# A hybrid decoder layer: weight rooms at other addresses, convolution taps spread over two steps, four rooms for the first token tiles, dt later

## The reference

```python
u = rms_norm(x, norm_pre_w)                          # (2048, 1024)
proj = u @ w_in                                      # q k v g z x b c dt
q, k, v, g, z, xbc, dt = split(proj)                 # 4*1024, 1024, 1024+512, 16
attn = mixture_of_dilations(q * 64**-0.5, k, v) * silu(g)   # windows 128, 512, 2048; dilations 1, 4, 16
xbc = silu(causal_depthwise_conv(xbc, conv_w) + conv_b)     # 4 taps along the tokens
dt = softplus(dt + dt_bias)
y = ssd_chunked(xs, dt, -exp(a_log), b, c) + d_skip * xs    # state-space scan, chunks of 128
y = gated_group_rms_norm(y, z, ssm_norm_w)
out = x + rms_norm(concat(attn, y) @ w_out, norm_post_w)
```

## Time and profile before

| | before |
|---|---|
| median of 3 runs | 2313.26 us (2310.68 to 2316.27) |
| profiled execution: time, span | 2307.99 us, 2306.2 us |
| mean granted clock of TensorE | 0.977 |
| TensorE matmuls busy | 2177.1 us, 94% |
| VectorE busy | 1413.7 us, 61% |
| ScalarE busy | 997.9 us, 43% |
| GpSimd busy | 1443.9 us, 63% |
| HBM over the span | 120 GB/s |

### The profile page before, as it was taken

How to read it: one execution, slowest core, us unless ns; L and a number is a source line. 1 busy time by engine, 2 the same in 40 slices (tenths; PEclk the granted TensorE clock), 3 DMA queues, 4 the chain that set the end, 5 groups by cost and what they waited for, 6 DMA issues and landing times. The chain is left out here.

```text
span 2306.2 us, 34733 instructions
## 1 busy us (share of the span) xinstructions
PE 2177.1 (94%) x12061; PEld 1835.2 (80%) x12061; DVE 1413.7 (61%) x2605; ACT 997.9 (43%) x2341; POOL 1443.9 (63%) x877
## 2 busy tenths in 40 slices
PE   5999999989999999998989999999996699999998
PEld 3778877777888888877858999999996588888876
DVE  6462236995522223499657777777777866666661
ACT  5332343333422234333336777777774423323231
POOL 6577677888667767788815556556542455555552
PEclk8999999999999999999989999999998799999999
DMA  4463332333733233322455555565547343444431
GB/s 129 151 230 105 92 106 61 108 92 128 237 107 108 97 92 110 92 73 83 137 126 114 144 126 133 139 158 137 139 115 260 103 130 128 138 129 131 140 100 55
DMA packets 260220, 287.19 MB, mean 125 GB/s; under 512 B 78420, under 2 KB 228112, under 8 KB 251984
## 3 DMA queue, kind: packets, MB, share of 16 engines
q1 hardware_dynamic: 258944, 277.50, 41.2%
q0 software_dynamic: 1104, 7.47, 0.8%
HBM read 195.28 MB, written 81.00 MB: 120 GB/s over the span
## 5 line engine op out<-in xcount | busy, mean ns | idle before, releaser
L935 PE MATMUL mm<-b_hi,w_hi 128*128 128x512 f32 x1456 | 576.3, 396 | 7.0 <-DVE fm L757 4.9
L937 PE MATMUL mm<-b_hi,w_lo 128*128 128x512 f32 x1456 | 573.0, 394 | 0.0
L936 PE MATMUL mm<-b_lo,w_hi 128*128 128x512 f32 x1456 | 572.5, 393 | 0.0
L493 POOL TENSOR_TENSOR w_lo<-w_raw,w_hi 128x512 fp32r<-128x512 f32 x208 | 315.3, 1521 | 132.1 <-ACT w_hi L567 123.9
L935 PEld LDWEIGHTS mm<-b_hi,w_hi 128*128 128x128 f32 x1456 | 274.0, 188 | 70.2 <-issue 9.4
L937 PEld LDWEIGHTS mm<-b_hi,w_lo 128*128 128x128 f32 x1456 | 273.9, 188 | 62.8
L936 PEld LDWEIGHTS mm<-b_lo,w_hi 128*128 128x128 f32 x1456 | 274.1, 188 | 61.3
L1729 PE MATMUL ps_t<-ident_b,probs 128*128 128x128 f32 x1136 | 214.6, 279 | 13.9 <-ACT probs L1660 6.8
L567 ACT ACTIVATE w_hi<-w_raw 128x512 fp32r<-128x512 f32 x208 | 129.2, 627 | 214.0 <-PE mm L937 209.2
L2214 PE MATMUL ps_out<-wo_hi,mix_hi 128*128 128x512 f32 x512 | 208.7, 408 | 1.3 <-ACT mix_hi L2165 1.3
L757 DVE SCALAR_TENSOR_TENSOR fm<-mm,u 128x512 f32<-128x512 f32 x120 | 92.0, 769 | 184.8 <-PE mm L937 184.6
(11 more groups left out here) (236 smaller groups left out, 4443.4 us busy)
## 6 DMA issues: line engine op xcount, KB each, us to landing
w_raw<-in_w_in_dram SPq DMA_DIRECT2D x52, 1024.0 KB, 5.7
feat<-fm SPq DMA_DIRECT2D x56, 512.0 KB, 5.5
tok<-tok_tile SPq DMA_DIRECT2D x52, 512.0 KB, 4.1
raw_q<-feat SPq DMA_DIRECT2D x32, 512.0 KB, 6.3
raw_k<-feat SPq DMA_DIRECT2D x32, 512.0 KB, 6.5
cum_b<-cum_scratch SPq DMA_DIRECT2D x16, 1024.0 KB, 7.8
cls_nat<-cls_out SPq DMA_DIRECT2D x64, 132.0 KB, 2.7
tok_tile<-in_x_dram SPq DMA_DIRECT2D x16, 512.0 KB, 3.8
```

The source lines that it names most:

```text
L493: pool.tensor_tensor(wl[o][:, :, :], source(o, n), wh[o][:, :, :].bitcast(F32), ALU.subtract)\
L935: pe.matmul(bank, w_hi[:, k, :], bh[o][:, k, :], start=(opens and k == 0), stop=False)
L936: pe.matmul(bank, w_hi[:, k, :], bl[o][:, k, :], start=False, stop=False)
L937: last = pe.matmul(bank, w_lo[:, k, :], bh[o][:, k, :], start=False, stop=(closes and k == KH - 1))
```

## The change

- **Rooms.** `TANH_AT` loses its 32 bytes, and with it all that is placed above it. Rooms 4 and 5 move to `SLOT_AT`, 112 KB. `dt_late` moves into the second half of a token room (T3).
- **Orders.** New strings put a v, k or q step behind most convolved steps. The feature set of each step is written out in `SETS`.
- **Taps.** The step behind a convolved one runs the first tile's four taps, tanh and finish, the step after that the second tile's (`conv_behind`). Each tile is turned by itself: `turn_at` is (n + 2, 0) and (n + 3, 0) for convolved steps, (n + 1, 3) for both tiles of v and z. `free_fm`, `turned` and `tok_made` count by tile.
- **Token tiles.** `x_room` has four rooms, two of them in `raw[1]`. Tiles 0 to 3 are loaded at once, 4 to 7 behind the first normalisations, and the second weights only behind the last turned part. `PREP` starts at step 0.
- **Reload.** Places (25, 1), (25, 3), (25, 4), (25, 6) and (26, 0) to (26, 2); six rows are loaded at step 24, sixteen at 25, six at 26 (ten, sixteen and two before).
- **dt.** `take_size` and `take_one_plus` run at s = 1 and s = 5, `take_ratio` at 5, `take_softplus` at 10, `cumulate` at 13; on ScalarE `dt_exps` at p = 2 and `dt_log` at p = 7.

```diff
-TANH_AT = CONV_AT + 8 * KB + 32
+TANH_AT = CONV_AT + 8 * KB
...
-ORDERS = ("qqqqkkvvvvzzzzxxxxbcggggkk", "qqqqkkkkvvvvzzzzxxxxbcgggg")
+ORDERS = ("qqqqxvxkxvxkbvckvzzzzggggk", "qxqxqxqxkbkckkvvvvzzzzgggg")
+SETS = ("00000101010101011010101010", "01010101010100010101010101")
...
-        self.set = 0 if n < 6 else n % 2
+        self.set = int(SETS[half][n % len(SETS[0])])
+        self.turn_at = [(n + 2 + b, 0) for b in range(2)] if self.conv else [(n + 1, 3)] * 2
...
+        SLOT_AT = sb.at
+        sb.at += 8 * KB
...
-        for rooms, group in ((sb, (4, 5)), ...
+        for rooms, group in ((Rooms(nc, SLOT_AT, SLOT_AT + 8 * KB), (4, 5)), ...
...
-        dt_out = [fm1[1], place(nc, "dt_late", dt_late_at, [P, HALF])]
+        dt_out = [fm1[1], place(nc, "dt_late", T3 * 16 * KB + 8 * KB, [P, HALF])]
+        x_wide = raw[1][:, :, :].rearrange("p k f -> p (k f)")
+        x_rooms = [*x_tok, x_wide[:, 0:D_MODEL], x_wide[:, D_MODEL:2 * D_MODEL]]
...
-        RELOAD = {(TURN - 1, 1): 0, (TURN - 1, 2): 1, (TURN - 1, 3): 2, (TURN - 1, 5): 3, (TURN, 0): 4, (TURN, 1): 5,
+        RELOAD = {(TURN - 1, 1): 0, (TURN - 1, 3): 1, (TURN - 1, 4): 2, (TURN - 1, 6): 3, (TURN, 0): 4, (TURN, 1): 5,
                   (TURN, 2): 6}
-        PREP = {j + 1: j for j in range(LANES)}
+        PREP = {j: j for j in range(LANES)}
...
+        def conv_behind(n):
+            if n and steps[n - 1].conv:
+                return steps[n - 1], 0
+            if n > 1 and steps[n - 2].conv:
+                return steps[n - 2], 1
+            return None
...
-                for i in range(2, 6):
-                    sp.wait_ge(normed, i - 1)
+                for i in range(4, HT):
+                    sp.wait_ge(normed, i - 3)
                     load_x(i)
-                load_w(1)
...
+                sp.wait_ge(u_turned, START)
+                load_w(1)
...
                     if conv:
-                        bring(conv)
+                        if conv[1] == 0:
+                            bring(conv[0])
                         for j in range(CONV_K):
-                            tap_step(conv, 0, j)
+                            tap_step(*conv, j)
...
                     read(s, A12, put(s, 0, 0), c1[:, :])
-                    if conv:
-                        tap_step(conv, 1, 0)
-                        tap_step(conv, 1, 1)
...
                     if conv:
-                        finish(conv, 0)
-                        tap_step(conv, 1, 2)
-                        tap_step(conv, 1, 3)
+                        finish(*conv)
...
-                        if s == 4:
+                        if s == 1:
+                            take_size()
+                        if s == 5:
+                            take_one_plus()
                             take_ratio()
-                        if s == 8:
+                        if s == 10:
                             take_softplus()
-                        if s == 12:
+                        if s == 13:
                             cumulate()
...
+                    if is_first(pair) and p == 2:
+                        dt_exps()
+                    if is_first(pair) and p == 7:
+                        dt_log()
```

More of the change, by code:

```diff
@@ L159, in all_steps @@
             out.append(Step(len(out), half, kind, FIRST_PAIR[kind] + order[:i].count(kind), out[:]))
+    for s in out:
+        s.turn = [sum(t.turns and t.turn_at[b] < s.turn_at[b] for t in out) for b in range(2)]
     return out
@@ L243, in project @@
         prep_out = sem("prep_out")
-        stage_in = [sem(f"stage_in{i}") for i in range(len(stage))]
+        rows_in = [sem(f"rows_in{i}") for i in range(len(stage))]
+        X_LOADS = [6, 6, 2, 2]
         u_turned = sem("u_turned")
@@ L267, in project @@
         conv_done = sem("conv_done")
-        turned = sem("turned")
-        tok_made = sem("tok_made")
+        turned = [sem(f"turned{b}") for b in range(2)]
+        tok_made = [sem(f"tok_made{b}") for b in range(2)]
         tok_out = [sem(f"tok_out{b}") for b in range(2)]
@@ L313, in bank, with due, free_fm @@
             return mm[(PRODUCTS * s.n + o) % BANKS]
-        def free_fm(eng, s):
+        def due(n, o):
+            return [(s, b) for s in steps if s.turns for b in range(2) if s.turn_at[b] == (n, o)]
+        def conv_behind(n):
[4 more added lines that the diff above has]
+            return None
+        def free_fm(eng, s, b):
             m = s.before
@@ L320, in free_fm @@
             if m is not None and m.turns:
-                eng.wait_ge(turned, 4 * (m.turn + 1))
+                eng.wait_ge(turned[b], 2 * (m.turn[b] + 1))
             if s.n == first_one:
@@ L359, in store_fm, with store_tok @@
                     sp.dma_start(dst, src).then_inc(fm_out[s.set], 16)
[L361 to L365, removed]
+                def store_tok(s, b):
+                    sp.wait_ge(tok_made[b], 2 * s.turn[b] + 2)
+                    sp.dma_start(tok_view[:, s.half * HT:(s.half + 1) * HT, (s.pair * 2 + b) * P:(s.pair * 2 + b + 1) * P],
+                                 tok[b][:, :, :]).then_inc(tok_out[b], 16)
                 def store_rows(j):
@@ L422, in _ @@
                             store_fm(last, b)
[L423 to L426, removed]
+                    for part in due(n, 0):
+                        store_tok(*part)
                     if n in PREP:
@@ L653, in _ @@
                     square(i + 2)
[L654 to L657, removed]
+                    high(i, 0)
+                square(6)
+                square(7)
+                high(4, 0)
                 for j in range(LANES):
@@ L675, in _ @@
                             square(HT + 2 * PREP[n] + half)
+                    conv = conv_behind(n)
                     if n:
                         read_first(s)
[L678 to L682, removed]
+                    high(0, n + 1)
+                    for part in due(n, 0):
+                        collect(*part)
                     reload(n, 0)
                     high(1, n + 1)
[L685 to L688, removed]
                     reload(n, 1)
@@ L697, in _ @@
                     high(4, n + 1)
-                    if last is not None and last.conv:
-                        conv_tanhs(last, 1)
+                    reload(n, 4)
                     high(5, n + 1)
-                    reload(n, 5)
                     high(6, n + 1)
+                    reload(n, 6)
                     if s.gz:
@@ L859, in _ @@
                     last = steps[n - 1] if n else None
-                    conv = last if last is not None and last.conv else None
+                    conv = conv_behind(n)
                     if n in PREP:
@@ L1053, in _ @@
                             multiply(s, o)
-                        if o == 0 and last2 is not None and last2.conv and last2.turns:
-                            turn_tiles(last2)
-                        if o == 0 and last is not None and last.kind == "v":
-                            turn_tiles(last)
-                        if o == 1 and last is not None and last.kind == "z":
-                            turn_tiles(last)
+                        for part in due(n, o):
+                            turn_tile(*part)
                         reload(n, o)
```

170 lines of the change are left out of this document (90 added, 80 removed).

## The result

The changed kernel takes 2249.88 us (median of 4 runs, 2247.75 to 2251.10) against 2314.56 for the kernel before in the same runs; the ratio is 0.9722, with a 95% interval of 0.9705 to 0.9739. In a second comparison it was 2250.65 against 2310.79, 0.9739 (0.9726 to 0.9753). So it is 60 to 65 us faster; the prediction was 2255.7, a gain of 57.6.

The account below looks back on a forecast made before the run. TensorE was taken as full outside the convolved stretches and VectorE as the bound of the steps behind convolved ones; the terms sum to -57.6 from the 2313.26 median, giving 2255.7 us, range 2243 to 2268 (8 in 10: 2241 to 2280).

Parts of the forecast that it names:

- Rooms, -16: Weight rooms moved to whole KB: 208 of 364 products 0.07 to 0.08 us faster, 13 to 17 us over 52 steps.
- rival 1: Address plays no part; products are slow by their place in the step: gain 38.1 us, time 2275, chance 0.09.
- Output projection, -3.5: Stretch 1850 to 2290: wo_lo tiles leave the slow addresses, 0.11 us per call over 32 calls, 0 to -4.5.
- Convolved stretches, -34.9: Steps around the convolved ones: taps spread over two steps let 24 tile steps fit, removing losses of 17.1 and 17.8 us.
- rival 2: GpSimd becomes the bound, stretching to 20.6 us in each of 24 tile steps: time 2287, chance 0.10.
- Switches, +0.8: Turning each tile by itself makes 10 more switches between products and transposes, about 0.08 us each.
- the z turn, -1.4: The first z turn's wait of 1.4 us at step 11 goes away, being asked for later in the step.
- Startup, -7: Four rooms for the first token tiles remove VectorE's two waits for late tiles: 7 us less, between -2.7 and -11.
- Preparation, +1.4: Tokens of the other half: three TensorE waits grow by 0.3 us each and preparation starts earlier; 0 to +4.
- Reload, +1: Token-part reload: same transposes at other products, two rows loaded a step later; 1 us more, 0 to +3.
- dt later, +2: Start of attention: no gain counted, two table loads of 1.28 us less a slack of 1; -1 to +5.
- VectorE's dt work is only moved: Claim within the attention term that moving dt shifts VectorE's dt work by one to four units.

Follow-up runs that it names:

- two-room kernel: The changed kernel with the startup of before (two rooms for the token tiles, second weights early), preparation still from step 0: 2253.48 us, 0.9750 of the kernel before.

## Why the prediction was right, and where not

The time came out 5.8 us under the forecast and within its range; in spans the gain was 60.2 for 57.6. The large terms were right in mechanism and size. Part of the closeness is luck: startup, preparation and reload together gave 3.4 less than forecast, and attention 4.0 more, by a mechanism that the forecast did not have. Point by point:

- **Rooms, -16.** A plain step gives 0.32, so 52 steps give 16.6. Size and cause were right, the rule behind it was not: I wrote "an odd multiple of 32 bytes"; what the runs show is the distance between weights and moving operand modulo 256. The experiment with the rooms alone gave 14.2 with the output projection in it, since a third of the steps was then bound by something else: the term was right only beside the others. The chance of 0.09 for rival 1 is answered by that experiment.
- **Output projection, -3.5.** 0.11 us per call, and 3.5 from the first matmul of the first call to the end (486.8 to 483.3).
- **Convolved stretches, -34.9.** All waits there are gone; of the projection's 53.8 us the other terms leave 34.9 for it. VectorE's 16.25 per tile step for 16.3 forecast, GpSimd's 18.10 for 17.3; rival 2 (GpSimd the bound) was 1.9 us per step away. The read of product 1 at 11.5 for 11.4; the slack was 3.0 where I had 2.4, because product 5 comes behind the transposes.
- **Switches, +0.8, and the z turn, -1.4.** 0.03 per pair of turns, so +0.3 to +0.4; the z turn waits no more.
- **Startup, -7.** 5.3 in the profile (66.77 to 61.52 and 83.46 to 78.15), so mis-sized by 1.7. In the profile of the second comparison it is 3.0 at step 1, and the two-room kernel is only 2.8 to 3.6 slower in the medians. So the true size may be half of the forecast. Step 0 begins 1.7 later; that this is because more token tiles share the first transfers is argued, not tried.
- **Preparation, +1.4.** Waits of 5.5 for 4.9, and 1.7 at half clock behind the longest; steps 1 to 4 take 84.3 where 83.1 less 1.3 was the forecast's base, so +2.5.
- **Reload, +1.** Steps 25 and 26 take 52.1 for 51.1 in spite of 0.6 from the rooms, so +1.6; one gap of 1.36 is new (at 614.2), for which the profile names nobody.
- **dt later, +2.** The first head takes 51.4 for 53.1, so -1.8, and without the move it takes 54.4: -3. The step that failed is "VectorE's dt work is only moved". Forecast was a loss of 2, measured a gain of 1.8 to 3. The wait of 5 us for a copy behind `cumulate` went with the move, leaving one of 2.15; the table loads, priced at +1.6, cost TensorE 1.36, and the wait for dt's transfer, which comes before them, fell into the 9.95 us in which TensorE waits for v anyway.

The projection gave 53.8 of the 60.2, for 56.1 forecast; attention gave 2.0 where a loss of 2 was forecast, the start of the last stage 0.9 for which there was no term, and its calls 3.5.

The runs decide on the rules cited. The Trainium skill ("TensorE: Matmul & The Clock Gate", Step-by-step) has two independent read ports, and by it the rooms would change nothing. The kernel with the rooms alone went from 233 to 227 ns, so the measurement decides against reading it that way: the pace depends on how the two operands lie to each other. That the weight load takes its share from the running matmul is one possible cause; no run shows it. The drain that the Trainium skill ("ScalarE: Activation LUTs", What ACT_TABLE_LOAD costs) adds to a table load does not show in the changed kernel either: the activation behind each of the two loads starts 0.02 us after it, and the two leave a gap of 1.36 on TensorE.

## What to carry to other kernels

Where a stream of matmuls runs at an odd pace, list the pace by the room of each operand, and try weights and moving operands at the same address modulo 256 bytes; that was shown here for one shape and type. Vector work that stands behind a step's reads is worth spreading over the next steps before it is made faster: its order in front of the read that frees a PSUM bank, not its sum alone, sets the wait. A load that is moved back in a queue must be followed to whoever waits for it in order: a chain that was hidden behind another wait is not free.

## What the runs showed of the hardware

- Matmuls of 128x128 by 128x512 in fp32r run 226.7 ns apart when weights and moving operand lie at the same address modulo 256 bytes (distances 0 and 256 tried), and 233 ns apart at distances of 32, 64, 80, 128 and 224, whichever of the two is shifted. If only one of the two weight tiles of a product is off by 32, the product runs at 232.9; with one at 96 and one at 128 it runs at 230.6, which fits no theory here. Other distances and other types were not tried by themselves.
- Behind a slow product a clean one sometimes starts slow, for about seven matmuls (product 5 of the kernel with tiles at 128 and 256, 47 of 49 steps), and sometimes does not (product 6 of the kernel before, none of 44). When it does is open.
- Behind a wait of 2.7 us the next eight matmuls ran at the 1.2 GHz level (436 ns apart, granted clock 0.51), and in the kernel with four more taps 5 to 13 did behind 13 of 16 waits of 3.4 us and more (417 to 427 ns). One of 3.4 there (in 253.6 to 257.0, granted clock 1.00) and one of 2.3 in the kernel with two more taps were followed by none, nor were those of 1.6 us and less in steps 1 and 3 of the changed kernel.
- An activation behind a table load of 1.28 us starts 0.02 us after it, at both loads of the changed kernel's first head.
